# A tuned FP32 encoder trunk in which ScalarE's second-pair copies go ahead of a silu, a row tile's addition moves forward, and one output tile is begun inside its predecessors

## Reference

```python
def conv_ffn(h, past_f, w_up, conv_w, w_down):
    z = h @ w_up
    g, up = jnp.split(z, 2, axis=-1)
    gc, new_past_f = causal_dwconv(g, past_f, conv_w)
    return (jax.nn.silu(gc) * up) @ w_down, new_past_f

for l in range(DEPTH):
    h = rmsnorm(x, norm_mix[l])
    ...                                   # y = mixer_ab or mixer_c of h
    x = x + y
    h = rmsnorm(x, norm_ffn[l])
    y, pf = conv_ffn(h, past_f[l], w_up[l], conv_f_w[l], w_down[l])
    x = x + y
```

## Time and profile before

| | us |
|---|---|
| median of 3 runs | 2156.5 |
| lowest, highest | 2152.11, 2157.8 |
| profiled execution, its own time | 2156.07 |
| span of that execution in the trace | 2154.3 |

### The profile page before, as it was taken

The page is one execution under the profiler, slowest core; times in us unless marked ns, Lnnn a source line. Parts: engine busy times, 40 slices in busy tenths (PEclk is TensorE's granted clock), DMA queues, the critical chain, the costliest instruction groups (busy, mean ns, idle before and its releaser), DMA issues. The chain is left out here.

```text
span 2154.3 us, 36509 instructions
## 1 busy us (share of the span) xinstructions
PE 2109.9 (98%) x15464; PEld 2096.3 (97%) x15464; DVE 1529.6 (71%) x1872; ACT 733.7 (34%) x1128; POOL 941.4 (44%) x592
## 2 busy tenths in 40 slices
PE   9999999999999999999999999999999999999997
PEld 8999999999999999999999999999999999999997
DVE  5999679676666666665987576796766666766667
ACT  5564155322223322223633222453222232322233
POOL 2866244434334443334455344444344444443343
PEclk9999999999999999999999999999999999999998
DMA  4111310111111111111111111101111111111112
GB/s 162 44 37 41 122 50 30 61 39 60 41 59 59 50 34 56 50 50 54 45 40 51 48 59 40 50 30 59 40 59 40 59 59 42 38 59 44 56 42 81
DMA packets 34002, 115.38 MB, mean 54 GB/s; under 512 B 3824, under 2 KB 7408, under 8 KB 33840
## 3 DMA queue, kind: packets, MB, share of 16 engines
q1 hardware_dynamic: 33840, 113.06, 15.6%
HBM read 108.42 MB, written 4.62 MB: 52 GB/s over the span
## 5 line engine op out<-in xcount | busy, mean ns | idle before, releaser
L625 PE MATMUL psum<-xs_hi,w_hi 128*128 128x264 f32 (+2 forms) x3784 | 1105.2, 292 | 23.2 <-DVE work L2162 6.1
L627 PE MATMUL psum<-xs_hi,w_lo 128*128 128x264 f32 (+2 forms) x3784 | 1101.7, 291 | 0.0
L626 PE MATMUL psum<-xs_lo,w_hi 128*128 128x264 f32 (+2 forms) x3784 | 1098.6, 290 | 0.0
L1063 POOL TENSOR_TENSOR w_lo<-raw,w_hi 128x512 fp32r<-128x512 f32 (+1 forms) x415 | 665.1, 1615 | 884.5 <-ACT w_hi L1234 760.5
L625 PEld LDWEIGHTS psum<-xs_hi,w_hi 128*128 128x128 f32 x3784 | 713.8, 189 | 29.9 <-DVE work L2162 7.4
L626 PEld LDWEIGHTS psum<-xs_lo,w_hi 128*128 128x128 f32 x3784 | 713.4, 189 | 0.0
L627 PEld LDWEIGHTS psum<-xs_hi,w_lo 128*128 128x128 f32 x3784 | 713.2, 188 | 0.0
L625 PE MATMUL psum<-act_hi,w_hi 128*128 128x352 f32 x1200 | 388.6, 324 | 3.0 <-POOL w_lo L1071 1.5
L627 PE MATMUL psum<-act_hi,w_lo 128*128 128x352 f32 x1200 | 388.1, 323 | 0.0
L626 PE MATMUL psum<-act_lo,w_hi 128*128 128x352 f32 x1200 | 385.5, 321 | 0.0
L1234 ACT ACTIVATE w_hi<-raw 128x512 fp32r<-128x512 f32 x383 | 234.0, 625 | 310.1 <-PE psum L627 276.0
(11 more groups left out here) (222 smaller groups left out, 1934.8 us busy)
## 6 DMA issues: line engine op xcount, KB each, us to landing
raw<-slabs SPq DMA_DIRECT2D x188, 512.0 KB, 3.3
x<-x_t SPq DMA_DIRECT2D x16, 528.0 KB, 6.4
y_t<-x SPq DMA_DIRECT2D x4, 600.0 KB, 3.1
y_t<-x SPq DMA_DIRECT2D x2, 400.0 KB, 2.5
x<-mix SPq DMA_DIRECT2D x1, 512.0 KB, 3.3
y_t<-x SPq DMA_DIRECT2D x1, 512.0 KB, 2.9
y_t<-x SPq DMA_DIRECT2D x2, 256.0 KB, 2.7
x<-bs SPq DMA_DIRECT2D x1, 256.0 KB, 3.7
```

What stands on the lines that cost most here:

```text
L625: nc.tensor.matmul(out, w_hi[:, w], hi, start=start, stop=False, skip_group_check=reopen)
L626: nc.tensor.matmul(out, w_hi[:, w], lo, start=False, stop=False, skip_group_check=reopen)
L627: return nc.tensor.matmul(out, w_lo[:, w], hi, start=False, stop=stop, skip_group_check=reopen)
L1063: nc.gpsimd.tensor_tensor(w_lo[:, slab], src, w_hi[:, slab].bitcast(F32), ALU.subtract).then_inc(weights_ready, 1)
```

## The change

Three things are changed.
1. In the second pair of stages 1 and 3, ACT's silu of the first pair moves from ahead of the copies "entry 5, L1530, entry 6" to behind them. DVE takes the order of the other pairs: product and C11 ahead of C22 and C21.
2. In all stages, DVE's third `combine` moves from ahead of tile 7's addition to behind the last sum of squares. `combined_low` of it moves behind the first slab sums of the second pair, `mean_square` moves ahead of the last `combined_low` and `make_t1`. ACT's last `make_b22` and the third `t_high` move behind the four weight copies of the first pair; POOL's third `t4_lo` moves behind the low parts of entries 2 and 3.
3. In the join of stage 1, PE does 18 of the matmuls of tile 2 (k = 0 to 2, columns 0 to 703) between input k = 2 and input k = 3 of tiles 0 and 1, in PSUM banks 6 and 7. The wait for slab 1 of the weights moves with them. The rest of tile 2 follows at its old place.

No matmul, copy or addition is added or taken away; their order alone changes.

```diff
--- before.py
+++ after.py
@@ -175,7 +175,7 @@
 
 def pair_read(p, unit, which):
 
-    if unit == ("pair", 0, 1):
+    if p == 2 and unit == ("pair", 0, 1):
         which = {C22_READ: 1, C21_READ: 2, C11_READ: 3, C12_READ: 4}[which]
     return PLACES[p][unit][1] + which
 
@@ -451,6 +451,8 @@
 
         X_BANKS = (0, 6)
         Y_BANK, Z_BANK = 2, 4
+
+        THIRD_BANK = X_BANKS[1]
 
         def halves_of(bank):
             return psum[:, bank:bank + 2, 0:PART]
@@ -967,7 +969,14 @@
             def join(p, unit):
 
 
+
                 acts = ACT0[p] + 2 * unit[1] - 2
+
+                def third_tile(k):
+                    for c in range(2):
+                        split_product(psum[:, THIRD_BANK + c, 0:CH], tile_at(ring(p, unit, 1), k), ah[k][:, chunk(c)],
+                                      al[k][:, chunk(c)], k == 0, k == 3)
+
                 for m in range(KD):
                     if m % 2 == 0:
                         pe.wait_ge(weights_ready, step_of(p, unit, m // 2) + 1)
@@ -981,6 +990,19 @@
                                 last = down_tile(i, slab, 4 * i + k, k, k, 4)
                                 if k == 3:
                                     last.then_inc(tile_done, 1)
+                            if p == 1 and k == 2:
+                                pe.wait_ge(weights_ready, step_of(p, unit, 1) + 1)
+                                pe.wait_ge(tile_evacuated, pair_read(p, ("pair", unit[1], 1), C12_READ))
+                                for early in range(3):
+                                    third_tile(early)
+                    elif p == 1 and m == 2:
+                        third_tile(3)
+                        down_banks_free(p, unit, m)
+                        cols = chunk(2)
+                        for k in range(4):
+                            last = split_product(psum[:, 2, 0:REST], tile_at(slab, k), ah[k][:, cols], al[k][:, cols],
+                                                 k == 0, k == 3)
+                        last.then_inc(tile_done, 1)
                     elif m > 1:
                         down_banks_free(p, unit, m)
                         for k in range(4):
@@ -1134,10 +1156,10 @@
                 last_lo(p, 3)
                 t4_lo(s, 1)
                 entry_lo(p, 0, 0, 0, 1)
+                entry_lo(p, 0, 0, 2, 3)
                 if p == 1:
                     pool.wait_ge(stored, 16)
                 t4_lo(s, 2)
-                entry_lo(p, 0, 0, 2, 3)
                 t4_lo(s, 3)
 
             def t4_lo(s, kp):
@@ -1405,13 +1427,15 @@
                     elif m > 2:
                         act.wait_ge(early_sum, POOL_SUMS * p + m - 2)
                     nc.scalar.activation(t_sq[m], x_t[:, m, :], ACT.Square).then_inc(square_ready, 1)
-                    if m % 2:
+                    if m in (1, 3, 5):
                         make_b22(p, m // 2)
-                    elif m:
+                    elif m in (2, 4):
                         t_high(p, m // 2 - 1)
                     if m == 5:
                         entry_hi(p, 0, 0, 0, 1)
                 entry_hi(p, 0, 0, 2, 3)
+                make_b22(p, 3)
+                t_high(p, 2)
 
             def make_b22(p, kp):
                 if kp:
@@ -1521,7 +1545,7 @@
                     hidden_hi(p, b - 1, 0)
                 elif q == 0 and b >= 2:
                     hidden_hi(p, b - 1, 1)
-                if p != 2 and before[0] == "pair":
+                if p != 2 and before[0] == "pair" and before != FIRST:
                     silu_gate(p, before[1], before[2])
                 entry_hi(p, b, q, 5)
                 act.wait_ge(tile_done, group_done(p, b, q, 2))
@@ -1529,6 +1553,8 @@
                     act.wait_ge(c_gated, 1)
                 nc.scalar.activation(two(half(up, 0)), halves_of(x_bank), ACT.Copy).then_inc(part_copied, 1)
                 entry_hi(p, b, q, 6)
+                if p != 2 and before == FIRST:
+                    silu_gate(p, 0, 0)
                 if p == 2 and q == 0:
                     hidden_hi(p, b - 1, 1)
                 act.wait_ge(tile_done, group_done(p, b, q, 3))
@@ -1635,14 +1661,15 @@
                                          hi_t[:, m, :].bitcast(F32), ALU.mult,
                                          ALU.subtract).then_inc(xg_ready, 1)
 
-            def add_down(done, before, pset, m, loaded=None):
+            def add_down(done, before, pset, m, loaded=None, first_banks=None):
 
                 if loaded is not None:
                     dve.wait_ge(x_loaded[m], loaded)
                 dve.wait_ge(tile_done, done)
 
                 dve.wait_ge(tile_evacuated, before)
-                dve.tensor_tensor(wide(x_t[:, m, :]), wide_banks(pset), wide(x_t[:, m, :]), ALU.add)
+                banks = wide_banks(pset) if first_banks is None else first_banks
+                dve.tensor_tensor(wide(x_t[:, m, :]), banks, wide(x_t[:, m, :]), ALU.add)
                 dve.tensor_tensor(x_t[:, m, chunk(2)], rest_bank(pset), x_t[:, m, chunk(2)],
                                   ALU.add).then_inc(tile_evacuated, 1)
 
@@ -1650,7 +1677,8 @@
                 add_down(job + 1, evacuated(job - 1), job % 2, m, loaded=32)
 
             def ff_add(p, unit, m):
-                add_down(down_done(p, unit, m), down_read(p, unit, m) - 1, m % 2, m)
+                banks = psum[:, THIRD_BANK:THIRD_BANK + 2, 0:CH] if unit == JOIN[1] and p == 1 and m == 2 else None
+                add_down(down_done(p, unit, m), down_read(p, unit, m) - 1, m % 2, m, first_banks=banks)
 
             def mean_square(p, sums):
                 dve.wait_ge(stats_ready, p + 1)
@@ -1938,7 +1966,7 @@
                     add(m)
                     if m >= 1:
                         normed_low(p, m - 1)
-                    if m in (2, 4, 6):
+                    if m in (2, 4):
                         combine(p, m // 2 - 1)
                     if m in (3, 5):
                         combined_low(p, m // 2 - 1)
@@ -1946,7 +1974,7 @@
                         square_sum(p, m - 1)
                 normed_low(p, KD - 1)
                 square_sum(p, KD - 1)
-                combined_low(p, 2)
+                combine(p, 2)
 
             def square_sum(p, m):
                 dve.wait_ge(square_ready, KD * p + m + 1)
@@ -2015,11 +2043,12 @@
                 g = conv_in
                 dve.wait_ge(squares_summed, DVE_SUMS * (p + 1))
                 clear_history(g)
+                sums(p, 0, 1, 1)
+                combined_low(p, 2)
                 combine(p, KP - 1)
-                sums(p, 0, 1, 1)
+                mean_square(p, psum[:, 7, 0:ROW_TILES])
                 combined_low(p, KP - 1)
                 make_t1(p)
-                mean_square(p, psum[:, 7, 0:ROW_TILES])
                 sums(p, 0, 1, 2)
                 sums(p, 0, 1, 3)
                 dve.wait_ge(r_ready, 2 * (p + 1))
@@ -2167,12 +2196,10 @@
                     dve.tensor_tensor(two(half(up, 0)), halves_of(Z_BANK), two(half(up, 0)),
                                       ALU.add).then_inc(tile_evacuated, 1)
 
-                if before == FIRST:
+                if p == 2 and before == FIRST:
                     sums(p, after[1], after[2], 1, step_of(p, unit, 4))
                     c22()
                     c21()
-                    if p != 2:
-                        product(p, 0, 0)
                     c11()
                     sums(p, after[1], after[2], 2)
                 else:
```

## The result

| | before | changed |
|---|---|---|
| median, us | 2154.93 (22 runs) | 2157.34 (22 runs) |
| lowest to highest, us | 2151.71 to 2157.8 | 2154.9 to 2160.41 |
| profiled execution, its own time and span, us | 2156.07, 2154.3 | 2156.04, 2154.3 |

The ratio is 1.0013, 95% interval 1.0007 to 1.0019: 1.5 to 4.1 us slower. The forecast was 2156, "no change" with a sum of -0.2 us; the time is inside its range, but the kernel did become slower by a little, and 22 runs can tell that. So the waits have to be compared one by one.

What follows compares the result with a forecast made beforehand. PE was busy 2109.9 of 2154.3 us, so only waits between matmuls could change. Terms -7.4 - 2.6 + 6.6 + 2.2 + 1.0 = -0.2 us on 2156.07 gave 2156 us, no change, within 2151 to 2160.

Steps and rivals of the forecast that it cites:

- C22 of the second pair: Stages 1 and 3, DVE behind the silu: some 5 us of work, hidden with under 1 us to spare, no wait.
- the wait ahead of tile 4: Join of stage 1, weight slab 2 late: +1.0 us taken, 0.5 us or up to 2.1 if combine keeps POOL out.
- The four waits of the silu: Second and third pair, stages 1 and 3: waits of 0.94, 1.17, 0.87, 0.93 us gone but for 0.2; -7.4 us for both.
- L1646's 2.6 us: PE's waits for tile 7's addition in the passages into the three stages, forecast to go: -2.6 us.
- the gate copy: First gate copy in each of three passages, late behind the fourth combine: new wait of 2.2 us each, +6.6 us.
- join: End of stage 1: PE waits 4.25 us for slab 1's low part instead of 2.05 for k = 3, +2.2 us.
- C22 of the third pair: Stages 1 and 3: wait of 0.93 us forecast to shrink to an estimated 0.2 us, a gain of 0.73.
- the clock: Rival, chance 0.10: PE's clock falls at new waits of 2.2 us or more, 1.65 us each; 2163.7 us.

Runs made afterwards that it cites:

- e10: Kernel before with only the silu change (change 1), but the high copy of weight entry 6 put behind the silu; 2148.53 us, ratio 0.9973.
- e6: Changed kernel with C22 of the second pair moved ahead of the second slab sum on DVE; 2157.38 us, ratio 1.0011 to before.
- e3: Kernel before with only the join change (18 matmuls of tile 2 ahead of k = 3); 2160.66 us, ratio 1.0025.
- e2: Kernel before with only the second change (tile 7's addition ahead of the third combine); 2159.9 us, ratio 1.0024.
- e5: Changed kernel with ACT's first gate copy moved ahead of the fourth t_high; 2151.57 us, ratio 0.9985 to before.
- e8: Changed kernel with the second pair's first slab sums on DVE back behind the fourth combine; 2151.97 us, ratio 0.9989 to before.
- e4: Kernel before with the join change, and ACT's copy of weight slab 1 moved ahead of the last pair's silu; 2155.18 us, ratio 1.0004.
- e1: Kernel before with only the silu change (first pair's silu behind the copies, DVE in the other pairs' order); 2147.81 us, ratio 0.9961.
- e9: Kernel before with the silu and combine changes, no join change, gate copy ahead of fourth t_high, slab sums behind fourth combine; 2141.49 us, ratio 0.9945.
- e11: Changed kernel with gate copy and join slab 1 and 2 copies earlier, slab sums behind fourth combine, C22 unmoved; 2142.68 us, ratio 0.9952 to before.

## Why the prediction was wrong

**The step that failed** is in part 1: C22 of the second pair, "Hidden too, with under 1 us to spare". It is 1.3 us late, twice: 2.6 us of waiting that the sum has at nothing, the largest of its misses. With this, part 1 gives 5.2 us by its brackets, not 7.4. That its time still came out at -7.0 us is luck: the 0.26 us per wait, for which the sum has no term either, made up for it. Timelines of DVE and POOL of the changed kernel there:

```profile
372.90 1.68 DVE L1698 TENSOR_SCALAR work<-work,const 128x1058 f32<-128x1058 f32 x1
...
377.21 1.79 DVE L1944 TENSOR_TENSOR raw<-raw 128x512 f32<-128x512 f32 x1
...
380.86 0.71 DVE L2184 TENSOR_TENSOR work<-psum,slots_lo 128x528 f32<-128x528 f32 x1
...
382.41 1.77 DVE L1949 TENSOR_TENSOR raw<-raw 128x512 f32<-128x512 f32 x1
384.10 0.69 DVE L2191 TENSOR_TENSOR work<-psum,work 128x528 f32<-128x528 f32 x1
```

```profile
369.47 4.54 POOL L1085 TENSOR_TENSOR w_lo<-raw,w_hi 128x512 fp32r<-128x512 f32 x3 [1.36 <-ACT w_hi L1256]
...
376.06 2.39 POOL L1085 TENSOR_TENSOR w_lo<-raw,w_hi 128x512 fp32r<-128x512 f32 x1 [2.05 <-ACT w_hi L1256]
...
379.60 4.03 POOL L1085 TENSOR_TENSOR w_lo<-raw,w_hi 128x512 fp32r<-128x512 f32 x2 [1.15 <-ACT w_hi L1256]
```

I read what C22 has ahead of it off the third pair and took off the 2.69 us that DVE stood there, as if the rows that remain kept their length. In the second pair each of three DVE rows on C22's path, which is a tap and two slab sums, meets a low part of POOL and takes 0.9 to 1.1 us longer than its plain 0.77 or 0.68 us. The last of the three was in what I read off (1.75 us in the third pair); the other two are new. The tap makes the silu end about 0.9 us later. The first slab sum holds the product up: it starts 1.0 us behind the silu's end, where in the third pair it follows at once, and from that end (378.50) to C22's end (384.79) it is 6.3 us instead of "some 5". Together they use up the "under 1 us to spare" and 1.3 us more. The weight copies on either side of the silu had moved with part 1, and I costed them at nothing. e10 shows that putting one back isn't enough, e6 that moving C22 removes this wait and passes most of it on to the next pair. So the wait is settled as one of DVE's order and its collisions; how much either of the first two collisions adds by itself was not measured.

**The second miss** is one of size: the wait ahead of tile 4 is 1.99 us, not 1.0 (2.04 in e3). The forecast had an upper end of 2.1 us, for DVE's `combine` keeping POOL out. The number came true by another route. DVE and POOL of the changed kernel, timelines:

```profile
1031.49 2.99 DVE L1996 SCALAR_TENSOR_TENSOR work<-x,const,work 128x528 f32<-128x528 f32 x1
```

```profile
1030.32 3.60 POOL L1108 TENSOR_TENSOR r_rows<-r_rows,work 128x1056 f32<-128x1056 f32 x1 [11.86 <-ACT work L1429]
1033.88 2.81 POOL L1085 TENSOR_TENSOR w_lo<-raw,w_hi 128x1024 fp32r<-128x1024 f32 x1
```

The slab's low part ends at 1036.69 and starts only behind a sum of squares that POOL needs 3.60 us for. Before, that sum took 2.47 us (L1086, 1027.43). I had weighed `combine` against the low part, not this sum; here it is `combine` that stands 2.99 us behind POOL.

**What held.**
- The four waits of the silu: gone in both stages, the last of them wholly (0.2 us left for it was too much, 0.4 us in the sum).
- Part 2: L1646's 2.6 us gone, and the gate copy late in all three passages. The fourth `combine` was forecast to end at 354.1; it ends at 353.76. Timeline of DVE of the changed kernel:

```profile
343.55 1.80 DVE L1996 SCALAR_TENSOR_TENSOR work<-x,const,work 128x528 f32<-128x528 f32 x1
345.38 1.68 DVE L1998 SCALAR_TENSOR_TENSOR work<-x,const,work 128x528 f32<-128x528 f32 x1
347.10 0.77 DVE L2002 SCALAR_TENSOR_TENSOR work<-x,const,work 128x528 f32<-128x528 f32 x1
347.79 0.69 DVE L1944 TENSOR_TENSOR raw<-raw 128x512 f32<-128x512 f32 x1
...
349.00 2.25 DVE L1706 TENSOR_TENSOR xs_lo<-work,xs_hi 128x528 fp32r<-128x528 f32 x2
351.38 0.77 DVE L1996 SCALAR_TENSOR_TENSOR work<-x,const,work 128x528 f32<-128x528 f32 x1
```

  POOL's low parts fell on the third `combine` as forecast (1.80 and 1.68 us); POOL's `t4_lo` met `combined_low` (2.25 us for two) and not the fourth `combine`. The sum of the steps is the same. At full clock the wait is 2.4 to 2.6 us (e2, e6), forecast 2.2; where it shows as 0.9 to 1.1 us, the clock had fallen just ahead of it (next section). e5 and e8 undo two different causes of it and give 5.8 and 5.4 us.
- Part 3: 4.25 us, no wait for k = 3, and the cause, the place of the slab's copy on ACT (e4).

**The sum again**, from the waits of the two traces: silu -7.8 + 2.6, addition -2.6, gate copy +2.9, join +2.2, tile 4 +2.0: -0.7 us. Eleven waits went and six came, at 0.26 us each: -1.3 us. Between 300 us and the tail, the trace of before has two stretches at half clock, that of the changed kernel four; each costs 1.5 us (last section): +3.0 us. That makes +1.0 us. It can be read directly, between two places that both kernels pass. Timelines of PE, before and then the changed kernel:

```profile
275.30 2.38 PE L763 MATMUL psum<-ident,tail_hi 128*128 128x128 f32 x18
...
2122.83 0.79 PE L1009 MATMUL psum<-one,r_rows 128*100 128x1 f32 x8
```

```profile
274.73 2.38 PE L765 MATMUL psum<-ident,tail_hi 128*128 128x128 f32 x18
...
2123.30 0.78 PE L1031 MATMUL psum<-one,r_rows 128*100 128x1 f32 x8
```

1847.53 us before and 1848.57 in the changed kernel: +1.04 us. So the account closes for these two executions. It isn't the +2.4 us of the medians, as the stretches differ from one execution to the next. With equal stretches on both sides and the gate copy at the 2.5 us of full clock, three times, the waits give -5.2 - 2.6 + 7.5 + 4.2 - 1.3 = +2.6 us. That is an estimate and fits the medians, but no run shows how many stretches the other executions had.

Against that estimate, the forecast's -0.2 misses +2.6 (C22 of the second pair), +1.0 (tile 4), +0.9 (the gate copy, 7.5 and not 6.6), -0.4 (C22 of the third pair) and -1.3 (the cost of each wait beyond its bracket). For the clock the forecast took no change. Its rival "the clock" had it fall behind new waits of 2.2 us or more. That is seen twice in e2 and twice in e6, but not in the changed kernel's trace, where the stretches at the gate copy stood ahead of the waits and shortened them. Nor does every wait of this length bring one: behind the join's 2.05 us, which the forecast priced with 1.65 us for the clock, e1 and e2 have the granted clock at 1.00.

## What to carry to other kernels

When an order is taken over from one stage to another, the durations don't come with it: for each row on the path look at what the engine that holds it up does at that moment in the new order (here a tap of 0.77 us took 1.68 and a slab sum of 0.68 us took 1.79). Count the waits as well as adding them up: each cost 0.26 us beyond its bracket. When work is put off behind one deadline, the next one on that queue is what counts, and the short copy that PE waits for should go first (e5: 5.8 us for one moved line). And a change of several parts is judged by its parts: here one gave 7 us and two cost 5.1 and 5.8 us, and with two lines put right and one part left out (e9) it is 12 us faster than before.

## What the runs showed of the hardware

**The clock can take a wait's place.** Windows of the changed kernel, PEclk third from last: the passage into stage 1, then the same place in stage 3.

```profile
346.00:350.00 4.00, 4.00 (x37) 3.97 (x36) 3.96 (x6) 3.40 (x7) 1.81 (x2) 1.00 0.63 233
350.30:353.70 3.40, 3.40 (x19) 3.40 (x17) 3.20 (x6) 2.04 (x4) 0.00 (x0) 0.53 0.02 8
...
1432.30:1435.70 3.40, 3.40 (x18) 3.40 (x17) 3.20 (x5) 2.11 (x5) 0.38 (x1) 0.53 0.37 140
```

PE falls from 2.4 to 1.2 GHz at 350.3, with no idle time ahead of it. What it had done just before is in this row of its timeline: 18 matmuls of a single column.

```profile
347.44 1.99 PE L680 MATMUL psum<-one,r_rows 128*128 128x1 f32 x18
```

In stage 2, from the start of these 18 matmuls to that of the last one ahead of the gate copy, PE takes 4.83 us in e2 (1069.10 to 1073.93, no stretch) and 6.36 us in the changed kernel (1071.92 to 1078.28, with one): a stretch costs 1.5 us. PE then waits 1.08 us, where e2 has 2.60. In e2 the clock fell behind the wait (0.53 above). A wait of 1 us behind a slow stretch is no smaller loss than one of 2.6 us. Whether a stretch comes at such a place differs between kernels whose order there is the same: in the passage into stage 3 it came in the kernel before, at 1429.6, and not in e1. The profiled executions of e1 and e11 have none at all until the tail, and PE is busy 2102.2 and 2100.8 us there instead of 2109.9. How often each comes over many executions can't be told from one profile per kernel. What makes the clock fall here was not tested: no run changed the 18 matmuls.

**DVE and POOL hold each other up for whole instructions.** POOL's 3.60 us from 1030.32 end at 1033.92; DVE's `combine` row beside it, issued at 1031.49, takes 2.99 us, which is the 2.43 us until then and little less than its plain 0.77 us. A row that reads one operand from PSUM (L2184, at 380.86) keeps its 0.71 us while POOL is in the low part that it began at 379.60. That agrees with the Trainium skill ("SBUF — State Buffer", section "Who interferes with whom"), by which a VectorE instruction with two SBUF inputs and a GpSimd instruction that reads SBUF exclude each other for the whole instruction. By that rule the prediction had each of the gate copy's waits at 3.4 us and by the rows at 2.2; it is 2.4 to 2.6. The three collisions of the changed kernel in the passage into stage 1 cost 1.0, 0.9 and 0.9 us (1.80, 1.68 and 2.25 us instead of 0.77, 0.77 and 1.31), not 1.3 each; that the low parts had begun before DVE's row was issued, so that only their rest was waited for, would explain it and was not tested.
